# Delta rule: the norm's row difference ahead of the hats on VectorE, the norm's other steps and the keys' sums of squares some products further back

## What is computed

```python
def _rwkv7(z, s0, w0, w2, a0, a2, g2, k_k, k_a, r_k, lnx_g, lnx_b):
    ...
    kk = (k * k_k).reshape(hs)
    kk = kk / jnp.maximum(jnp.sqrt(jnp.sum(kk * kk, axis=-1, keepdims=True)), L2_EPS)
    ...
    def step(S, inp):
        r_t, w_t, k_t, v_t, kk_t, a_t = inp
        sa = jnp.einsum('bhvk,bhk->bhv', S, -kk_t)
        S = (S * w_t[:, :, None, :] + sa[..., None] * (kk_t * a_t)[:, :, None, :]
             + v_t[..., None] * k_t[:, :, None, :])
        return S, jnp.einsum('bhvk,bhk->bhv', S, r_t)
    ...
    mu = jnp.mean(y, axis=-1, keepdims=True)
    var = jnp.mean(jnp.square(y - mu), axis=-1, keepdims=True)
    y = ((y - mu) * lax.rsqrt(var + GN_EPS)).reshape(bsz, seq_len, D_RWKV) * lnx_g + lnx_b
    bonus = jnp.sum(r4 * k4 * r_k, axis=-1, keepdims=True) * v4
    y = (y + bonus.reshape(bsz, seq_len, D_RWKV)) * g
    return y, s_last
```

## Time and profile before

| | before |
|---|---|
| median of 3 runs | 3587.78 us |
| profiled execution, its own time | 3578.63 us |
| its span | 3576.8 us |
| TensorE busy | 3291.8 us (92%) |
| VectorE busy | 2000.4 us (56%) |
| ScalarE busy | 1172.5 us (33%) |
| GpSimd busy | 547.6 us (15%) |
| mean granted clock of TensorE | 0.957 |

### The profile page before, as it was taken

One profiled execution on the slowest core, in us unless ns is written; L12 is line 12 of the kernel. 1 busy time (PEld: TensorE's weight loads), 2 busy tenths in 40 slices (PEclk: granted clock), 3 DMA queues, 4 the chain that ended last, 5 costly groups with the idle time before them and its releaser, 6 DMA issues.

```text
span 3576.8 us, 78015 instructions
## 1 busy us (share of the span) xinstructions
PE 3291.8 (92%) x33400; PEld 3153.3 (88%) x33400; DVE 2000.4 (56%) x3597; ACT 1172.5 (33%) x2299; POOL 547.6 (15%) x499
## 2 busy tenths in 40 slices
PE   5898999869999998959999999999999999999998
PEld 5797897568888887858999999999999999999997
DVE  4414098156666665436555556765555566655565
ACT  3223321144444443323222224522222354222234
POOL 2111120043333333121010003100100130000001
PEclk9998999979999999869999999999999999999999
DMA  3133121111111111043222224323322442222223
GB/s 120 49 114 107 44 80 56 50 50 30 29 29 30 29 29 21 26 151 115 87 71 75 66 71 139 111 77 104 103 75 71 122 123 77 87 82 75 66 82 116
DMA packets 414063, 272.05 MB, mean 76 GB/s; under 512 B 37008, under 2 KB 404112, under 8 KB 413584
## 3 DMA queue, kind: packets, MB, share of 16 engines
q1 hardware_dynamic: 413744, 267.27, 24.7%
HBM read 230.70 MB, written 37.57 MB: 75 GB/s over the span
## 4 chain that ended last, share of the span: by engine, by line
PE 50%; DVE 3%; ACT 1%; DMA 1%; issue 1%; SPq 0%; POOL 0%; POOLq 0%; DVEq 0%; ACTq 0%
PE oe_pg L699 14%; PE oe_pd L727 14%; PE oe_pv L699 14%; PE oe_pg L760 4%; PE oe_pd L747 2%; DVE oe_w_lo L509 1%; PE oe_pv L767 1%; DMA oe_raw<-in_w_out 0%; DVE oe_rms L540 0%; ACT oe_w_hi L360 0%; DVE oe_x L525 0%; DMA oe_raw<-in_w_ple 0%; DVE oe_xs_lo L535 0%; DVE oe_h L516 0%; PE oe_pn L688 0%
## 5 line engine op out<-in xcount | busy, mean ns | idle before, releaser
L509 DVE TENSOR_TENSOR oe_w_lo<-oe_raw,oe_w_hi 128x1024 fp32r<-128x1024 f32 (+1 forms) x294 | 382.1, 1310 | 118.9 <-ACT oe_w_hi L360 93.1
L516 DVE TENSOR_TENSOR oe_h<-oe_pd,oe_h 128x352 f32<-128x352 f32 x576 | 292.4, 522 | 186.5 <-PE oe_pd L727 141.4
L2338 PE MATMUL fr_bk<-fr_xs,fr_ring 128*128 128x352 f32 (+2 forms) x2016 | 343.5, 333 | 17.8 <-DVE fr_xs L2199 10.3
L2338 PEld LDWEIGHTS fr_bk<-fr_xs,fr_ring 128*128 128x128 f32 x2016 | 336.0, 195 | 23.4 <-issue 14.8
L727 PE MATMUL oe_pd<-oe_f_hi,oe_w_hi 128*128 128x352 f32 x1056 | 343.3, 325 | 8.1 <-DVE oe_h L516 8.1
L699 PE MATMUL oe_pg<-oe_xs_hi,oe_w_hi 128*128 128x352 f32 x1056 | 342.2, 324 | 6.7 <-DVE oe_xs_lo L530 6.6
L360 ACT CAST oe_w_hi<-oe_raw 128x1024 fp32r<-128x1024 f32 (+1 forms) x294 | 312.3, 1073 | 96.8 <-DMA oe_raw<-in_w_out 42.9
L727 PE MATMUL oe_pd<-oe_f_lo,oe_w_hi 128*128 128x352 f32 x1056 | 341.0, 323 | 0.0
L727 PE MATMUL oe_pd<-oe_f_hi,oe_w_lo 128*128 128x352 f32 x1056 | 340.9, 323 | 0.0
L699 PE MATMUL oe_pg<-oe_xs_lo,oe_w_hi 128*128 128x352 f32 x1056 | 340.3, 322 | 0.0
L699 PE MATMUL oe_pg<-oe_xs_hi,oe_w_lo 128*128 128x352 f32 x1056 | 340.3, 322 | 0.0
(11 more groups left out here) (381 smaller groups left out, 7095.6 us busy)
## 6 DMA issues: line engine op xcount, KB each, us to landing
oe_raw<-in_w_gate SPq DMA_DIRECT2D x66, 512.0 KB, 3.9
oe_raw<-in_w_val SPq DMA_DIRECT2D x66, 512.0 KB, 3.9
oe_raw<-in_w_down SPq DMA_DIRECT2D x66, 512.0 KB, 3.7
oe_raw<-in_w_out SPq DMA_DIRECT2D x48, 512.0 KB, 4.0
oe_raw<-in_w_pg SPq DMA_DIRECT2D x48, 512.0 KB, 3.7
fr_raw<-in_w_in SPq DMA_DIRECT2D x72, 256.0 KB, 3.0
rw_Z<-scratch_zr SPq DMA_DIRECT2D x15, 903.0 KB, 5.3
oe_h<-in_xT SPq DMA_DIRECT2D x6, 1408.0 KB, 10.8
```

What stands on the lines that cost most here:

```text
L509: dve.tensor_tensor(w_view(kind, lo), w_view(kind, raw[i % 2]), w_view(kind, hi).bitcast(F32), ALU.subtract).then_inc(w_lo, 1)
L516: dve.tensor_tensor(hm, pd[sums[key] % 3][:, 0:TW], hm, ALU.add).then_inc(h_ready, 1)
L2338: mm = pe.matmul(out, lhsT, rhs, start=(k == 0 and p == 0), stop=(k == KD - 1 and p == 2))
```

## The change

Only numbers in the tables change, and one call is added at the end for the part that no half of the samples does any more. On VectorE `d` goes from behind number 13 to 12, ahead of the hats, which stand at 13; `inv` of the group norm from 19 to 21; `dn` from 2 to 3. On ScalarE `nrm` goes from 8 to 9, and the group norm's two parts from 14 to 15 and 18 to 20. On TensorE `ss` goes from 8 to 9, `g` from 5 to 7 in the second half, and `finish` parts 0 and 1 from 11 to 12 and 16 to 18; part 2 goes from 21 of the first half to 1 of the second.

```diff
--- before.py
+++ after.py
@@ -1232,7 +1232,7 @@
 
                 NEXT = [{3: ["kk"], 9: ["L", "t"], 12: ["inv"], 19: ["aa", "sg"]},
                         {4: ["kkn", "Lp"], 7: ["b", "kp"], 19: ["bonus"]}]
-                BEFORE = [{13: ["d"], 19: ["inv"]}, {2: ["dn"], 13: ["dg", "db"], 14: ["dbonus", "y"]}]
+                BEFORE = [{12: ["d"], 21: ["inv"]}, {3: ["dn"], 13: ["dg", "db"], 14: ["dbonus", "y"]}]
                 HATS = [{13: ["bT", "aT"], 14: ["kT"]}, {15: ["bT", "aT"], 16: ["kT"]}]
                 REST = ["dn", "dg", "db", "dbonus", "y"]
 
@@ -1371,8 +1371,8 @@
 
                 PLAIN = {"D2", "Dt2", "D4", "Dt4", "D8", "Bt", "Kt", "X", "Vt", "Z32", "Z64"}
 
-                NEXT = [{4: ["th"], 5: ["kk2"], 7: ["wt", "at"], 8: ["nrm"]}, {8: ["e"], 19: ["g"]}]
-                BEFORE = [{14: 0, 18: 1}, {}]
+                NEXT = [{4: ["th"], 5: ["kk2"], 7: ["wt", "at"], 9: ["nrm"]}, {8: ["e"], 19: ["g"]}]
+                BEFORE = [{15: 0, 20: 1}, {}]
                 HATS_AT, ROWS_AT = [9, 17], [9, 16]
 
                 def half(t, q):
@@ -1593,8 +1593,8 @@
                         pe.wait_ge(prep_act, at(t + 2, PREP_ACT, "nrm"))
                     pe.matmul(side[1][:, 0:HP * W], bd64[:], yt[:, 0:HP * W], start=True, stop=True).then_inc(post_pe, 1)
 
-                NEXT = [{6: ["w"], 8: ["ss"], 20: ["spread"]}, {5: ["g"], 17: ["bonus"]}]
-                BEFORE = [{11: 0, 16: 1, 21: 2}, {}]
+                NEXT = [{6: ["w"], 9: ["ss"], 20: ["spread"]}, {7: ["g"], 17: ["bonus"]}]
+                BEFORE = [{12: 0, 18: 1}, {1: 2}]
 
                 def half(t, q):
                     before = (t, 0) if q else (t - 1, 1)
@@ -1616,6 +1616,7 @@
                     half(t, 0)
                     half(t, 1)
                 half(SAMPLES, 0)
+                finish(NB - 1, 2)
                 m = M[0]
                 pe.wait_ge(smp_in, 16 * DB)
                 wait_copied(pe, 1, NB - 1, "S")
```

## The result

The changed kernel takes **3536.53 us** (median of 4 runs, 3526.09 to 3541.13) against 3589.8 for the kernel before beside it: a ratio of 0.9846, 95% interval 0.9811 to 0.9881, faster by 53 us or 1.5%. The forecast was 3541. The profiled execution had a span of 3536.0 us, with TensorE at 93% of it.

A forecast was written before the change was run, and what follows sets the result against it. TensorE was taken to bound the delta rule, waiting 2.6 us a turn for ScalarE's square, then running slowly 1.4. Some 3.1 us over 14 turns (43) plus 4 gave 47: 3587.8 - 47 = 3541 us, range 3517 to 3574.

The forecast's parts named there:

- the walked turn: One delta-rule turn followed engine by engine: 45.00 us becomes 41.7, or 42.4 with 0.7 charged for slow clock.
- t1 behind GpSimd's d_r: VectorE's t1 waits out GpSimd's earlier shift d_r and ends at 1027.81 instead of 1027.11, delaying X3's add.
- The port: SBUF port shared by VectorE and GpSimd: t1 sits out exactly one GpSimd instruction, costing 0.70 us.
- The rival in which t1 sits out m_r too: X4 comes 1.1 us later, every turn keeps its slow stretch: 1.36 us a turn, about 3569; chance 0.18.
- d behind the norm step: On VectorE, the keys' norm step waits out GpSimd's z_r, then d runs 1030.4 to 1031.05, 1.9 us sooner.
- The spread in the second half: `finish` 2 moves 1.0 us of TensorE work at equal cost; its VectorE inverse is hidden by 1.1 us.
- the rival on the slower side: The inverse behind X64t's add is late for the spread and the second half waits: about 3627; chance 0.05.
- The gate's product: `g` behind Dt4 starts ScalarE's exponentials sooner, so D8's copy is no longer late for second-half X4: 0.4 us.
- The clock: A stretch at half clock behind the new 1.57 us idle, 1.4 us in every second turn: 0.7 a turn.
- The nearest row: Profile row of before: a TensorE wait of 1.44 us at 1453.17, followed by clock 0.50 from 1454.2 to 1457.5.
- The rival without any stretch: The new idle leaves the clock alone: 3.86 us a turn, 4.1 with kT early, about 3527; chance 0.19.
- The count and the rest: 14 turns preparing a full next block give 43 us; the samples' turn and half give 4 together.

The follow-up runs named there:

- the run with the root back: Changed kernel with the keys' root (`nrm`) put back at 8 on ScalarE, ahead of the copies of D8, Y and vT: 3524.63 us, ratio 0.9834.
- the title's step: Row difference d moved ahead of the hats on VectorE (13 to 12); as the only edit to the kernel before: 3536.42 us, ratio 0.9868.
- root back, hats late: Changed kernel with `nrm` back at 8, plus the hats later on VectorE so that the adds on X pass them: 3523.19 us (one run).
- root back, row sums first: Changed kernel with `nrm` back at 8, plus the row sums (`finish` 0) at 11, ahead of X4: 3517.61 us (one run).
- root back, both: Changed kernel with `nrm` back at 8, plus row sums ahead of X4 and hats later on VectorE: 3502.16 us, ratio 0.9762.

## Why the prediction was right

The mechanism held step by step; the gain was forecast at 47 us and came out at 53. The steps of the walked turn, in us from the scan:

| step | predicted | measured |
|---|---|---|
| t1 behind GpSimd's d_r | lasts 1.39 | 1.41 |
| X4, with TensorE idle before it | 4.13, idle 1.57 | 4.13, idle 1.40 by the view |
| row sums | 4.63 | 4.74 |
| d | 6.3 | 6.08 |
| sums of squares | 8.8, no wait | 8.96, no wait |
| Z64 | 10.07, wait 0.2 | 10.06, no wait (the sums end there) |
| AqkT | 10.57 (2.9 less) | 10.58 (2.92 less) |

- **The port.** The 0.70 taken for t1 was measured at 0.72, and the run with the root back shows its price in the turn: 0.59. The Trainium skill, "SBUF — State Buffer", section "Who interferes with whom", says that a VectorE instruction with two SBUF inputs and a GpSimd instruction that reads SBUF shut each other out, the first one for its whole length; by that rule t1 sits out d_r, and the trace agrees (0.69 alone, 1.41 behind d_r). The rival in which t1 sits out m_r too did not come.
- **d behind the norm step.** That step took 0.72 for eight columns and its end was 5.92 us behind the scan (982.67), the end of z_r being 5.90: it sat out z_r as the walk had it, and d came 0.2 earlier than predicted. Nothing waits for it.
- **The spread in the second half.** No wait stands there in the list of after; the 1.1 us of cover was enough, and the rival on the slower side did not come.
- **The gate's product.** Taken at 0.4, measured by its own run at 0.49: the wait for D8's copy went in full, so nothing of it was left to X3's add. The quiet turn is 41.46, not 41.7. Of that 0.24, 0.02 lies up to AqkT, 0.14 from there to the second half's X4 (14.60 us became 14.06, where 0.4 was taken), and 0.08 behind it, which was not traced.
- **The clock.** Taken at 0.7 a turn, from a stretch in every second turn; measured about 0.44, from four turns in 13 at 1.44. The mean lies 0.57 above the quiet turn (42.03 - 41.46); the other 0.13 are turns that are longer for another reason, which the prediction did not charge and no run explains. The price of a stretch, 1.4 us, was right (42.91 or 42.90 against 41.46). The nearest row, one wait of 1.44 us with a slow stretch behind it, led to a share that was too high; the true one stands in no row of before. The rival without any stretch would have been 3527, and the result lies between.
- **The count and the rest.** The prediction took 14 turns of this kind, and the waits bear it out: the fourteenth wait of the earlier trace rows comes 9.6 us behind the scan at 1388.35, that of the last full block (512 columns, as all before it). Only the next scan is that of the samples, 256 columns wide:

```profile
1445.24 0.69 DVE L1107 TENSOR_TENSOR_SCAN rw_p_L<-rw_seg,rw_p_w 128x256 f32<-128x256 f32 x1
```

  The time between these two scans fell by 4.8 us (56.90 to 52.09), more than the 3.16 of a turn, since beside the wait that went a long wait for an X add, 11.25 us, became 10.22. For the turn that prepares the samples and the samples' half 4 us were taken; from the samples' scan on it was 1.7.

So 14 x 3.16 + 4 = 48.2 is the prediction's sum (47 as it was rounded), and 52.8 was measured: 13 turns with 0.37 too little (0.24 quiet, 0.13 above it), 1.7 too little in the fourteenth, 0.5 in the first turns, and 2.3 too much for the end. That the last offsets some of the others is luck.

What the prediction did not see is that the title's step would have done alone, without the wait of 1.4 us. It walked the change as one piece and did not ask for each part's own worth; it had the price of the moved root (0.70) in the walk, but not the question whether the root brings as much, which the run with it back answers with no.

## What to carry to other kernels

Price each part of a change alone and behind the others: parts that take away one wait are substitutes, and one of them may be pure cost. When a copy gets ready sooner, ask who starts on it; here it was GpSimd, ahead of a VectorE instruction that TensorE was waiting for. In a program of stages, compare the length of turns within the stage, not the total, since another stage can vary by more than the edit.

## What the runs showed of the hardware

**How often the clock falls goes with the order of the work.** Only two of the orders were profiled twice. Reading the granted clock in half-microsecond windows over the 13 turns gives the time at 0.50. Beside it stand TensorE's waits in one undisturbed turn, from its timeline (before: a turn as shown):

| kernel | waits in a turn, us | stretches | time at 0.50, us |
|---|---|---|---|
| before | 2.6, 0.7, 0.5, 0.5 | 13 | 61.5 |
| change, `g` back (two profiles) | 1.4, 0.5, 0.5, 0.2 | 7, 7 | 41.0, 34.0 |
| change, d back | 1.4, 0.6, 0.5, 0.2 | 7 | 27.5 |
| change (two profiles) | 1.4, 0.5, 0.2 | 4, 4 | 13.0, 13.5 |
| root back, hats late | 0.7, 0.3, 0.2 | 3 | 10.5 |
| before, d ahead of the hats | 0.7, 0.6, 0.5, 0.5, 0.2 | 2 | 7.0 |
| root back | 0.7, 0.5, 0.2, 0.2 | 1 | 3.5 |
| root back, row sums first | 0.8, 0.5, 0.2 | 1 | 3.0 |
| root back, both | 0.3, 0.2 | 0 | 0 |

A stretch was 3.0 to 3.5 us long, or 6.5 to 7.0. Five of the 13 in the kernel before were of the long kind, and their turns lasted 46.5 us and more against 45.0 of the shown one, which is why the mean there was 45.56. The change cut the time at half clock by some 48 us, which at 1.44 us for a stretch of 3.5 is about 20 of the 45.8 us that the turns gained (an estimate from the price in the changed kernel). Why a further wait of 0.5 us in the other half of the turn brings seven stretches instead of four, and doubles some, stays open.

**One stage in front varies by 13 us without any edit.** The first scan of the delta rule stands at 731 to 735 us in six profiles and at 744 to 751 in five others; the changed kernel has been in both groups (744.36 and 731.27). The window view of TensorE (length, busy, clock, DMA share, GB/s) for the same stretch of the projection in its first and its second profile:

```profile
594.00:630.50 36.50, 35.33 (x184) 0.50 0.02 5
```

```profile
594.00:630.50 36.50, 34.51 (x316) 1.00 0.02 5
```

The same kernel ran 36.5 us at half clock once and at full clock the other time. It is so in all eleven profiles: the five late ones have a stretch at 0.50 of 41 to 44 us that begins between 584 and 595 us, and in the six others it ends after 3 to 14 us. Why it lasts in some executions stays open. The spans of these two profiles, 3536.0 and 3524.8, lie 11 us apart; how much of the scatter between the runs of one kernel comes from this, no profile shows. The second profile and that of before had the same start (731.27 and 731.26): their spans differ by 52.0 us, the medians by 53.3.

**Eight columns can cost as much as hundreds.** The keys' norm step, 128 x 8, took 0.72 us while a GpSimd instruction ran, and ended 0.02 us behind it; the row difference over 512 columns took 0.68.
